# Ring slots released on read, S5 preparation between projections, and a blocked DeltaNet inverse

## The chip, the cores and the metric

One core of one Trainium2 chip runs the whole layer in one launch. The metric is the device time of that core in microseconds (us). The kernel before has a median of 3605.3 us over 3 runs (3603.2 to 3605.53).

## The reference, cut to what matters

The program is one layer on 256 tokens of width 2048, all in float32: a token mixer, a layer norm, a mixture of 32 experts and a second layer norm.

```
proj   = x @ w_in                                   # S5 input u, q, k, v, z, beta/decay, two gates
y_s5   = glu(gelu(diagonal state scan(u)))          # 128 groups, 64 states, (y@w_glu_a)*sigmoid(y@w_glu_b)
q,k,v  = silu(conv4(...)); q,k normalised
lower  = I + strict_tril((k*beta) k^T * decay)      # per head and chunk
sol    = lower^-1 [v*beta, k*beta*exp(g)]           # triangular solve
o      = chunked delta rule with state S; o = rmsnorm(o)*norm_w*silu(z);  y_dn = o @ w_dn_out
mix    = (gate_s5*y_s5 + gate_dn*y_dn) @ w_mix_out
h      = layer_norm(ALPHA*x + mix);  out = layer_norm(ALPHA*h + experts(h))
```

## The kernel before, in words

Activations stand transposed in SBUF (`xT`: 16 tiles of 128 by 256 tokens). Nearly all weights stream through a **ring of three slots** of 2 MB (`ring`, 16 by 256 columns a partition). SyncE issues every load, in one hand-written order. `load_slot` (its call site is L300 in the profile) waits until a PSUM bank that an earlier slot filled has been *taken* by VectorE or ScalarE, then issues. On TensorE `project`/`part` (L553) wait for slot and bank and multiply 32 tiles of 128x128 with 256 tokens. Each float32 matmul is two load-and-multiply pairs of instructions, so a slot is 64 of each.

The order of the stages:

- **Prologue.** Six loads count on one semaphore, `pro_loaded`, and TensorE waits for all six before its transposes of x (L528). Then come beta and decay logits (L533), a chain over VectorE and ScalarE that ends in `glog_ready`, two sums (L538, L539), and `prologue_done`, after which group 0 starts.
- **DeltaNet groups.** A loop of 8, each with 4 value heads and two chunks of 128 tokens (`c` = 0, 1). TensorE projects q, k and half of v (the front), and spreads the other half of v (slot 0), z0 (slot 1) and z1 (slot 2) over the waits of the rest. The inverse of `lower` is built by doubling over `LEVELS` = 7 levels: P = At·Ti (L609) into one bank per chunk, VectorE masks it to `Pm` (L1258), X = Tt·Pm (L616) and Pm·Tt (L618), VectorE subtracts both from `Ti` (L1262) and `Tt` (L1264). Each level works on full 128x128 blocks of 4 heads; two z0 matmuls stand after P and one z1 matmul after X. Then the inverse is applied (L630 to L655) and the output is normalised (L661).
- **S5 input and preparation.** All engines meet at `phase_done[0]`. Only then SyncE issues the S5 parameters and the first three of 8 u slots (copied out at L1027). After the last u slot VectorE prepares the state matrices (L1298 to L1374), TensorE transposes them in 16 banks of four (L692) and ScalarE copies them (L1050 to L1052).
- **Scan.** Four chunks of 64 steps. TensorE forms the inputs (L703, tiles of 32 rows), ScalarE spreads them, VectorE steps the state (L1397 to L1403), TensorE forms the outputs (L734). The gate and output projections of DeltaNet run on TensorE beside the scan (L553, L721).
- **GLU.** 8 iterations of three slots in banks 0, 1, 2. ScalarE takes two sigmoids (L1083, L1085), VectorE three products and sums (L1435 to L1441).
- **Mix.** After `phase_done[2]`, 8 slots of `w_mix` (L762), with x, the norm rows and the first expert units loaded between.
- **Router and experts.** 16 expert pairs joined in tiles of 64 columns (L849 to L907), with six 2 MB units in flight. The diff has no line in it.

Of the kernel before, what the change touches and what calls it, by code (L numbers as in the profile page):

```python
# [18 lines left out]
P = 128  # L19
# [9 lines left out]
LEVELS = 7  # L29
OFF_Q = 2048  # L30
# [37 lines left out]
def build(nc, x, w_in, conv_w, a_log, dt_bias, norm_w, w_dn, lam_re, lam_im, log_dt, b_re, b_im, c_re, c_im,  # L68
# [3 lines left out]
    with ExitStack() as ctx:  # L72
# [148 lines left out]
        turn_begun = sem("turn_begun")  # L221
# [24 lines left out]
        s5_loaded, s5_tr, s5_trc, s5_step = sem("s5_loaded"), sem("s5_tr"), sem("s5_trc"), sem("s5_step")  # L246
        uch_ready = sem("uch_ready")
# [39 lines left out]
        def _(sp):  # L287

            sp.dma_start(xtok, x[0].rearrange("(m p) d -> p m d", p=P)).then_inc(pro_loaded, 16)
            sp.dma_start(wbd, in_rows(w_in[:, OFF_BD:OFF_BD + 2 * H_V])).then_inc(pro_loaded, 16)  # L290
            sp.dma_start(cw[:, :, :], conv_w.rearrange("(j p) t -> p j t", p=P)).then_inc(pro_loaded, 16)
            sp.dma_start(arow, a_log.partition_broadcast(P)).then_inc(pro_loaded, 16)
            sp.dma_start(dtrow, dt_bias.partition_broadcast(P)).then_inc(pro_loaded, 16)
            sp.dma_start(normw, norm_w.rearrange("(p o) -> p o", o=1)).then_inc(pro_loaded, 16)

            def load_slot(buf, src, bank, taken):
# [5 lines left out]
            with sp.Fori(0, GROUPS) as g:  # L302
                for r, col in enumerate((OFF_Q + 256 * g, OFF_K + 256 * g, OFF_V + 512 * g, OFF_V + 256 + 512 * g,
                                         OFF_Z + 512 * g, OFF_Z + 256 + 512 * g)):
                    load_slot(r % RING, in_rows(w_in[:, ds(col, SC)]), r % 3, 2 * g + r // 3 + 1)
# [12 lines left out]
            with sp.Fori(0, 2) as q:
                for r in range(3):
                    load_slot((S_U + r) % RING, in_rows(w_in[:, ds(768 * q + 256 * r, SC)]), r, U_USE + q + 1)  # L320
            for r in range(6, 8):
                load_slot((S_U + r) % RING, in_rows(w_in[:, SC * r:SC * r + SC]), r % 3, U_USE + 3)
            with sp.Fori(0, 8) as c:
                load_slot(S_DN % RING, in_rows(w_in[:, ds(OFF_GDN + SC * c, SC)]), 0, DN_USE + 1 + c)
# [1361 lines left out]
```

## Time and profile before

| What | Value |
|---|---|
| median of 3 runs | 3605.3 us |
| profiled execution | 3604.39 us |
| its span | 3602.3 us |
| TensorE matmul busy | 3206.1 us (89%) |
| VectorE busy | 1047.1 us (29%) |
| ScalarE busy | 482.2 us (13%) |
| mean read from HBM | 183 GB/s |

The profiled execution has 2.1 us around its span. A line such as L553 is a line of the kernel before; a helper's line stands for all its callers. A busy TensorE can still be waiting within a matmul's modelled end, so stage lengths are read from start times.

### The profile page before, as it was taken

The numbers are of one execution on the slowest core, as the hardware profiler recorded it, in microseconds if no ns is written. First come the engines' busy times: TensorE is split into PE (matmuls) and PEld (weight loads), VectorE is DVE, ScalarE is ACT, GpSimd is POOL, SyncE is SP. The second block draws the span as 40 slices with busy tenths as digits, with TensorE's granted clock in tenths as the row PEclk, the third lists the DMA queues.
The fourth block names the chain that finished last, engine by engine and source line by source line (L and its number), as shares of the span: only waits on it lengthen the run. The fifth ranks groups of instructions, "written<-read, shape, count | busy, mean of one in ns | idle before, by whom it ended". The sixth has DMA issues, their size and how long they took to land.

```text
span 3602.3 us, 44020 instructions
## 1 busy us (share of the span) xinstructions
PE 3206.1 (89%) x17395; PEld 2437.7 (68%) x17395; DVE 1047.1 (29%) x2650; ACT 482.2 (13%) x632; POOL 106.8 (3%) x189
## 2 busy tenths in 40 slices
PE   6999999999997868787788787895899999999996
PEld 6988888888886757676676676685545445454542
DVE  1433433433423026465570000003111111121114
ACT  1121121121121021101100000000011101111111
POOL 1010010010010000000000000000000000000000
PEclk9999999999999888798898998897899999999998
DMA  5232232242230622232223334273499999999995
GB/s 148 71 116 93 70 116 70 80 130 70 70 116 9 178 94 94 68 99 83 80 94 117 97 113 140 87 275 117 192 406 410 396 409 396 410 409 396 409 396 212
DMA packets 325973, 660.87 MB, mean 183 GB/s; under 512 B 41840, under 2 KB 271344, under 8 KB 275440
## 3 DMA queue, kind: packets, MB, share of 16 engines
q1 hardware_dynamic: 325904, 659.85, 49.9%
q8 instruction: 56, 0.92, 0.1%
q14 instruction: 13, 0.11, 0.0%
HBM read 657.73 MB, written 2.10 MB: 183 GB/s over the span
## 4 chain that ended last, share of the span: by engine, by line
PE 60%; issue 16%; DVE 9%; DVEq 5%; DMA 3%; ACT 2%; SPq 1%; ACTq 1%; POOL 1%; POOLq 1%
PE bank L553 17%; PE bank L860 12%; PE bank L849 6%; PE bank L891 6%; PE bank L907 3%; PE bank L618 3%; PE bank L616 3%; PE bank L762 2%; DVE arena L1401 2%; DVE arena L1403 2%; PE bank L609 2%; DVEq L1400 2%; DMA arena<-in_w_glu_a_dram 2%; PE bank L734 1%; PE bank L703 1%
## 5 line engine op out<-in xcount | busy, mean ns | idle before, releaser
L553 PE MATMUL bank<-arena 128*128 128x256 f32 x5632 | 1285.1, 387 | 117.3 <-DMA arena<-in_w_glu_a_dram 71.0
L553 PEld LDWEIGHTS bank<-arena 128*128 128x128 f32 x5632 | 1081.0, 195 | 274.3 <-issue 90.4
L860 PE MATMUL bank<-arena 128*64 128x512 f32 x2048 | 442.2, 592 | 0.7 <-ACT arena L1119 0.7
L860 PEld LDWEIGHTS bank<-arena 128*64 128x64 f32 x2048 | 147.1, 137 | 292.5 <-issue 290.5
L721 PE MATMUL bank<-arena 128*128 128x256 f32 x1024 | 229.1, 387 | 19.9 <-DMA arena<-in_w_dn_out_dram 19.9
L849 PEld LDWEIGHTS bank<-arena 128*128 128x128 f32 x1024 | 224.8, 311 | 15.4 <-issue 12.2
L721 PEld LDWEIGHTS bank<-arena 128*128 128x128 f32 x1024 | 198.8, 195 | 49.5 <-DMA arena<-in_w_dn_out_dram 16.0
L849 PE MATMUL bank<-arena 128*128 128x128 f32 x1024 | 227.8, 384 | 3.1 <-DVEq L1594 3.1
L891 PE MATMUL bank<-arena 128*64 128x512 f32 x1024 | 223.3, 594 | 7.7 <-ACT arena L1129 7.7
L891 PEld LDWEIGHTS bank<-arena 128*64 128x64 f32 x1024 | 72.2, 137 | 148.4 <-issue 137.0
L1629 DVE TENSOR_TENSOR arena<-arena,bank 128x512 f32<-128x512 f32 x128 | 87.7, 687 | 198.6 <-PE bank L907 198.5
L1600 DVE TENSOR_TENSOR arena<-bank,arena 128x512 f32<-128x512 f32 x16 | 11.1, 692 | 458.6 <-PE bank L860 458.6
L609 PE MATMUL bank<-arena 128*128 128x128 f32 x896 | 123.9, 281 | 7.8 <-DVEq L1253 3.9
L762 PE MATMUL bank<-arena 128*128 128x256 f32 x512 | 115.4, 390 | 12.6 <-DMA arena<-in_w_mix_out_dram 12.6
L609 PEld LDWEIGHTS bank<-arena 128*128 128x128 f32 x896 | 112.4, 191 | 21.0 <-DVEq L1266 13.1
L1435 DVE TENSOR_TENSOR arena<-arena,bank 128x512 f32<-128x512 f32 x8 | 5.5, 689 | 413.9 <-ACTq L1086 413.9
L762 PEld LDWEIGHTS bank<-arena 128*128 128x128 f32 x512 | 100.3, 196 | 27.7 <-issue 13.3
L618 PE MATMUL bank<-arena 128*128 128x128 f32 x896 | 118.3, 275 | 0.0
L616 PE MATMUL bank<-arena 128*128 128x128 f32 x896 | 118.2, 275 | 0.0
L907 PE MATMUL bank<-arena 128*128 128x512 f32 x256 | 115.2, 593 | 2.5 <-DVEq L1613 1.8
L1262 DVE TENSOR_TENSOR arena<-arena,bank 128x512 f32<-128x512 f32 x112 | 77.1, 688 | 137.7 <-PE bank L618 137.7
L616 PEld LDWEIGHTS bank<-arena 128*128 128x128 f32 x896 | 113.3, 192 | 2.9
(277 smaller groups left out, 2264.7 us busy)
## 6 DMA issues: line engine op xcount, KB each, us to landing
arena<-in_w_in_dram SPq DMA_DIRECT2D x72, 2048.0 KB, 8.4
arena<-in_w_gate_dram SPq DMA_DIRECT2D x64, 2048.0 KB, 16.3
arena<-in_w_up_dram SPq DMA_DIRECT2D x64, 2048.0 KB, 13.3
arena<-in_w_down_dram SPq DMA_DIRECT2D x64, 2048.0 KB, 19.2
arena<-in_w_dn_out_dram SPq DMA_DIRECT2D x16, 2048.0 KB, 11.3
arena<-in_w_glu_a_dram SPq DMA_DIRECT2D x8, 2048.0 KB, 8.3
arena<-in_w_glu_b_dram SPq DMA_DIRECT2D x8, 2048.0 KB, 13.7
arena<-in_w_mix_out_dram SPq DMA_DIRECT2D x8, 2048.0 KB, 11.1
```

The lines of the kernel that those rows point to most:

```text
L553: last = mm(ps[bank][:, ct * T:ct * T + T], ring[:, buf, k, ct * P:ct * P + P], rhs[:, k, :], start=k == 0, stop=k == KD - 1)
L609: last = mm(ps[3 + 2 * c][:, a * P:a * P + P], At[:, c, a], Ti[:, c, a], start=True, stop=True)
L616: mm(ps[3 + 2 * c][:, a * P:a * P + P], Tt[:, c, a], Pm[:, c, a], start=True, stop=True)
L618: last = mm(ps[4 + 2 * c][:, a * P:a * P + P], Pm[:, c, a], Tt[:, c, a], start=True, stop=True)
L721: last = mm(ps[1][:, ct * T:ct * T + T], ring[:, buf, k, ct * P:ct * P + P], oT[:, half * KD + k, :], start=half == 0 and ct == 0 and k == ...
L762: last = mm(ps[bank][:, m * SC:m * SC + SC], mg[:, k, m * P:m * P + P], ring[:, buf, k, :], start=k == 0, stop=k == KD - 1)
L849: last = mm(ps[4 + b][:, k * P:k * P + P], h1[:, m, 4 * b + k::KD], Psel[:, m].rearrange("p o c -> p (o c)"), start=m == 0, stop=m == MT - 1)
L860: last = mm(ps[bank][CAP * o:CAP * o + CAP, :], xg[:, 4 * q + k, CAP * o:CAP * o + CAP], w[:, o, k], start=q == 0 and k == 0, stop=q == 3 ...
L891: last = mm(ps[4 + n][CAP * o:CAP * o + CAP, :], shT[:, k, CAP * o:CAP * o + CAP], unit[j % UNITS][:, o, n * 512:n * 512 + 512], start=k = ...
L907: last = mm(ps[(2, 3, 0, 1)[n % 4]][:, :], pwT[:, (n // 4) * P:(n // 4) * P + P], ysb[:, (n % 4) * 512:(n % 4) * 512 + 512], start=True, s ...
L1262: V.tensor_tensor(Ti[:, c], Ti[:, c], ps[3 + 2 * c][:, :].rearrange("p (a t) -> p a t", a=GV), ALU.subtract)
L1629: V.tensor_tensor(av, av, ps[(2, 3, 0, 1)[n % 4]][:, :], ALU.add).then_inc(sc_taken, 1)
```

## The change

- **Loads.** `load_slot` waits on `bank_ready` (the slot has been read) in place of `bank_taken`. x comes in two loads, then the logit weights and the first three ring slots, then biases, conv weights and norm weight, each with its own semaphore. The S5 parameters are issued before the u slots, during the last group; the C matrices after `phase_done[0]`. The first `w_dn` slot of each pair is released at half through `half_read`. Three `w_mix` slots are issued before `phase_done[2]`.
- **TensorE order.** Group 0's first projection runs ahead of the decay sums, which move to bank 7. The u slots follow the last group without the meeting of all engines. The S5 transposes stand between u slots 1 and 2, 5 and 6, 6 and 7.
- **Inverse.** Six levels work on the two 64x64 diagonal blocks, of which `Ti`, `Tt`, `Pm` keep only 64 columns; the seventh fills the off-diagonal block of a full `TtF`. A `sem_inc` of `solve_begun` stands after each wait.
- **GLU.** Even and odd iterations use banks 0 to 2 and 3 to 5.

```
@@ sync
-            sp.dma_start(xtok, ...).then_inc(pro_loaded, 16)      # and wbd, cw, arow, dtrow, normw
+            for m in range(MT):
+                sp.dma_start(xtok[:, m], xv[:, m]).then_inc(x0_loaded, 16)
+            sp.dma_start(wbd, ...).then_inc(wbd_loaded, 16)
+            for r in range(3):
+                sp.dma_start(ring[:, r], ...).then_inc(slot_loaded[r], 16)
+            sp.dma_start(dtrow, ...).then_inc(bias_loaded, 16)
+            sp.dma_start(arow, ...).then_inc(bias_loaded, 16)
+            sp.dma_start(cw[:, :, :], ...).then_inc(pro_loaded, 16)
+            sp.dma_start(normw, ...).then_inc(pro_loaded, 16)
-                sp.wait_ge(bank_taken[bank], taken)
+                sp.wait_ge(bank_ready[bank], read)
                 sp.sem_inc(load_free, 1)
...
-            sp.wait_ge(phase_done[0], 4)
             (lam_re, lam_im, log_dt, b_re, b_im, d_skip loads)
+            for r in range(3):
+                load_slot((S_U + r) % RING, ..., r, U_USE)
+            sp.wait_ge(phase_done[0], 4)
             (c_re, c_im loads)
+            for r in range(3, 8):
+                load_slot((S_U + r) % RING, ..., r % 3, U_USE + r // 3)
...
+            with sp.Fori(1, 8) as c:
+                load_glu(c)
+            for r in range(2):
+                load_slot((S_MIX + r) % RING, ..., r, MIX_USE[r])
+            load_slot((S_MIX + 2) % RING, ..., 2, MIX_USE[2])
             sp.wait_ge(phase_done[2], 4)
@@ tensor
-            pe.wait_ge(pro_loaded, 96)
-            pe.wait_ge(const_ready, 1)
+            pe.wait_ge(ident_ready, 1)
+            pe.wait_ge(x0_loaded, 32)
...
+            project(16, 0, 0, 0, xT)
+            pe.wait_ge(const_ready, 1)
+            pe.wait_ge(glog_ready, 1)
+            mm(ps[7][:, 0:64], upper, small[:, 128:192], start=True, stop=True)
+            mm(ps[7][:, 64:96], ones[:, :], glog[:, 0], start=True, stop=True).then_inc(gcum_ready, 1)
+            project(16, 1, 1, 0, xT)
+            project(16, 2, 2, 0, xT)
+            with pe.Fori(0, GROUPS - 1) as g:
+                group(g)
+                front(g + 1)
+            group(GROUPS - 1)
...
+                for lv in range(HALF_LEVELS):
                     for c in range(2):
                         pe.wait_ge(t_ready[c], 8 * g + lv + 1)
+                        pe.sem_inc(solve_begun, 1)
                         for a in range(GV):
-                            last = mm(ps[3 + 2 * c][:, a * P:a * P + P], At[:, c, a], Ti[:, c, a], ...)
+                            for b in (lower, higher):
+                                last = mm(ps[3 + 2 * c][b, a * HB:a * HB + HB], At[b, c, a, b], Ti[b, c, a], ...)
                         last.then_inc(p_ready[c], 1)
                     z0(16 + 2 * lv, 18 + 2 * lv)
                     for c in range(2):
                         pe.wait_ge(pm_ready[c], 7 * g + lv + 1)
+                        pe.sem_inc(solve_begun, 1)
                         (the same halving for Tt·Pm and Pm·Tt: 16 products of 64x64 for 8 of 128x128)
+                    z1(lv, lv + 1)
+                lv = HALF_LEVELS
+                (per chunk 4 products P of At[lower, .., higher]·Ti[lower], z0 x2, 4 products Pm[higher]·TtF[higher], z0 x2)
...
+            u_slot(0)
+            pe.wait_ge(o_ready, GROUPS)
+            pe.sem_inc(phase_done[0], 1)
+            u_slot(1)
+            pe.wait_ge(s5_lam_loaded, 48)
+            pe.wait_ge(s5_step, 1)
+            (3 transposes of spar)
+            for r in range(2, 6):
+                u_slot(r)
+            turn_wide(0, bwide, 2)
+            u_slot(6)
+            turn_wide(1, cwide, 3)
+            u_slot(7)
...
+            with pe.Fori(0, 4) as q:
+                for odd in range(2):
+                    glu_slot(2 * q + odd, 0, 0, GLU_USE, uT, odd)
+                    glu_slot(2 * q + odd, 1, 1, GLU_USE, uT, odd)
+                    glu_slot(2 * q + odd, 2, 2, GS5_USE, xT, odd)
@@ vector
-                for lv in range(LEVELS):
+                for lv in range(HALF_LEVELS):
...
-                        V.tensor_tensor(Ti[:, c], Ti[:, c], ps[3 + 2 * c][:, :]..., ALU.subtract)
-                        V.tensor_tensor(Tt[:, c], Tt[:, c], ps[4 + 2 * c][:, :]..., ALU.subtract)
+                        V.tensor_tensor(Ti[:, c], Ti[:, c], heads(3 + 2 * c), ALU.subtract)
+                        if lv < HALF_LEVELS - 1:
+                            V.tensor_tensor(Tt[:, c], Tt[:, c], heads(4 + 2 * c), ALU.subtract)
+                        else:
+                            for b in (lower, higher):
+                                V.tensor_tensor(TtF[b, c, :, b], Tt[b, c], heads(4 + 2 * c)[b], ALU.subtract)
                         dve.drain()
                         dve.sem_inc(t_ready[c], 1)
+                lv = HALF_LEVELS
+                (copy Pm[higher] out of PSUM; TtF[lower, c, :, higher] = -heads(4 + 2 * c)[lower])
```

`heads(bank)` is the first 256 columns of a bank as 4 heads of 64. `glu_slot` is `project` with bank `3 * odd + b` and a wait for `bank_taken` one iteration older. `turn_wide` holds the 32 transposes of one of the two matrices, as L692 before. ScalarE's copies (`take_u`, `take_wide`) follow the same order.

## Rows read from the trace of the kernel before

**Rows 1.** Windows by stage: us, busy (x count) per engine, PEclk, DMA share, GB/s

```profile
0.00:40.95 40.95, 13.80 (x100) 13.36 (x101) 4.27 (x11) 10.35 (x16) 9.17 (x42) 0.94 0.81 222
40.95:84.95 44.00, 44.00 (x193) 38.34 (x193) 6.98 (x16) 4.49 (x5) 7.16 (x14) 0.94 0.30 96
638.33:776.68 138.35, 136.78 (x815) 122.24 (x814) 54.27 (x100) 28.06 (x33) 12.13 (x18) 1.00 0.28 91
1150.30:1187.75 37.45, 0.14 (x1) 0.00 (x0) 2.73 (x3) 3.96 (x5) 0.00 (x0) 0.57 0.66 123
1187.75:1336.84 149.09, 122.92 (x580) 108.36 (x580) 22.52 (x47) 15.21 (x29) 0.00 (x0) 0.90 0.44 139
1336.84:1908.66 571.82, 454.32 (x3585) 400.59 (x3585) 331.44 (x1311) 78.00 (x86) 0.00 (x0) 0.86 0.28 89
1908.66:2333.90 425.24, 354.25 (x1536) 306.00 (x1536) 14.52 (x21) 19.16 (x23) 0.00 (x0) 0.90 0.33 104
...
2344.34:2462.20 117.86, 115.41 (x512) 100.23 (x512) 4.81 (x7) 0.00 (x0) 0.00 (x0) 0.96 0.68 245
...
2547.70:3602.30 1054.60, 1011.42 (x4448) 502.46 (x4448) 196.60 (x366) 125.54 (x199) 0.00 (x0) 0.99 0.93 379
```

**Rows 2.** Timeline of TensorE in the prologue: start us, us, operation, idle before

```profile
18.66 5.38 PE L528 MATMUL bank<-ident,arena 128*128 128x128 f32 x32 [18.66 <-DMA small<-in_dn_norm_w_dram]
24.82 7.36 PE L533 MATMUL bank<-arena 128*128 128x64 f32 x64 [0.79 <-DVE arena L1175]
38.31 0.69 PE L538 MATMUL bank<-small,masks 128*128 128x64 f32 x2 [6.13 <-DVEq L1189]
```

**Rows 3.** DMA issues in the first 60 us: count, KB, us to landing

```profile
arena<-in_w_in_dram SPq DMA_DIRECT2D x3, 2048.0 KB, 14.8
arena<-in_x_dram SPq DMA_DIRECT2D x1, 2048.0 KB, 7.6
```

**Rows 4.** Timeline of TensorE in the inverse of group 4

```profile
672.78 2.29 PE L609 MATMUL bank<-arena 128*128 128x128 f32 x16
674.91 1.03 PE L553 MATMUL bank<-arena 128*128 128x256 f32 x4
675.77 1.05 PE L616 MATMUL bank<-arena 128*128 128x128 f32 x8
...
679.78 2.30 PE L609 MATMUL bank<-arena 128*128 128x128 f32 x16
...
707.79 2.29 PE L609 MATMUL bank<-arena 128*128 128x128 f32 x16
...
715.97 1.13 PE L630 MATMUL bank<-arena 128*128 128x128 f32 x8 [0.59 <-issue]
```

**Rows 5.** Timeline of VectorE in group 4

```profile
648.23 0.42 DVE L1238 COPY arena<-bank 128x256 f32<-128x256 f32 x1 [2.88 <-PE bank L571]
...
677.76 0.69 DVE L1262 TENSOR_TENSOR arena<-arena,bank 128x512 f32<-128x512 f32 x1 [1.96 <-PE bank L618]
```

**Rows 6.** Timeline of TensorE where it works on part of the array

```profile
1336.84 2.01 PE L703 MATMUL bank<-masks,arena 32*128 32x64 f32 x64 [2.48 <-DVE masks L1384]
...
2562.64 27.69 PE L860 MATMUL bank<-arena 128*64 128x512 f32 x128 [0.68 <-ACT arena L1119]
...
2589.73 0.60 PE L860 MATMUL bank<-arena 128*64 128x512 f32 x2
2590.26 1.57 PE L849 MATMUL bank<-arena 128*128 128x128 f32 x6
```

**Rows 7.** Timeline of TensorE: S5 transposes, and one scan output

```profile
1325.05 9.31 PE L692 MATMUL bank<-ident,arena 128*128 128x128 f32 x64 [23.69 <-DVEq L1370]
...
1609.15 12.42 PE L734 MATMUL bank<-arena 128*32 128x64 f32 x256 [9.53 <-DVEq L1407]
```

**Rows 8.** Waits from 1908 to 2463 us: us in total, times, longest

```profile
PE bank L553 <- DMA arena<-in_w_glu_a_dram: 71.0, 7, 10.3
...
PE bank L762 <- DMA arena<-in_w_mix_out_dram: 12.6, 2, 10.2
```

More of the change, by code:

```diff
@@ L29 @@
 LEVELS = 7
+HALF_LEVELS = 6
+HB = 64
 OFF_Q = 2048
@@ L294, in _, with load_slot @@
-            sp.dma_start(normw, norm_w.rearrange("(p o) -> p o", o=1)).then_inc(pro_loaded, 16)
-            def load_slot(buf, src, bank, taken):
-                sp.wait_ge(bank_taken[bank], taken)
+            def load_slot(buf, src, bank, read):
+                sp.wait_ge(bank_ready[bank], read)
                 sp.sem_inc(load_free, 1)
                 sp.dma_start(ring[:, buf], src).then_inc(slot_loaded[buf], 16)
[L302 to L305, printed above, removed]
@@ L318, in _ @@
[L318 to L324, printed above, removed]
-                for h in range(2):
-                    load_slot((S_DN + 1 + h) % RING, tile_rows(w_dn[h * D:h * D + D, ds(SC * c, SC)]), 1,
-                              DN_USE + 1 + c)
@@ new lines, in load_gdn, with load_dn_second @@
+            def load_gdn(c, bank, read):
+                load_slot(S_DN % RING, in_rows(w_in[:, ds(OFF_GDN + SC * c, SC)]), bank, read)
+            def load_dn_second(c, read):
+                load_slot((S_DN + 2) % RING, tile_rows(w_dn[D:2 * D, ds(SC * c, SC)]), 1, read)
+            load_gdn(0, 2, U_USE + 2)
+            load_slot((S_DN + 1) % RING, tile_rows(w_dn[0:D, 0:SC]), 0, U_USE + 3)
+            load_dn_second(0, U_USE + 3)
+            with sp.Fori(1, 8) as c:
+                load_gdn(c, 0, DN_USE + c)
+                sp.wait_ge(half_read, c)
+                sp.sem_inc(load_free, 1)
+                sp.dma_start(ring[:, (S_DN + 1) % RING], tile_rows(w_dn[0:D, ds(SC * c, SC)])).then_inc(
+                    slot_loaded[(S_DN + 1) % RING], 16)
+                load_dn_second(c, DN_USE + c)
@@ L466, in _ @@
             pool.drain()
+            for b in range(2):
+                rows = slice(HB * b, HB * b + HB)
+                g.tensor_copy(half_mask[rows], level_mask[rows, 0:HALF_LEVELS, HB * b:HB * b + HB])
+                g.tensor_copy(half_ident[rows], ident[rows, HB * b:HB * b + HB])
+            pool.drain()
+            g.memset(TtF, 0.0)
             g.tensor_copy(halfmask[:, 1:2], level_mask[:, 4, 0:1])
@@ L629, in _ @@
                 for a in range(GV):
-                    last = mm(ps[3][:, a * P:a * P + P], Tt[:, 0, a], vtok[:, 0, a], start=True, stop=True)
+                    last = mm(ps[3][:, a * P:a * P + P], TtF[:, 0, a], vtok[:, 0, a], start=True, stop=True)
                 last.then_inc(apply_pe, 1)
@@ L648, in _ @@
                 for a in range(GV):
-                    last = mm(ps[3][:, a * P:a * P + P], Tt[:, 1, a], R[:, a], start=True, stop=True)
+                    last = mm(ps[3][:, a * P:a * P + P], TtF[:, 1, a], R[:, a], start=True, stop=True)
                 last.then_inc(apply_pe, 1)
```

262 lines of the change are left out of this document (161 added, 101 removed).

## The prediction

> **What bounds the kernel now.** I cut the span by stage first (the windows view). In the group loop TensorE is busy 136.8 of a period of 138.35 us at the full clock of 2.4 GHz, VectorE 54.3 and ScalarE 28.1 [rows 1]: TensorE's own work is the bound there, eight times. Where the change moves loads it is not: TensorE stands still for 37.45 us before the u slots, is busy 122.9 of 149.1 us in S5 input and preparation, and 354 of 425 us in the GLU [rows 1]. In the scan TensorE waits for VectorE's last step (9.53 us before an output burst [rows 7]), so work taken from TensorE there buys nothing. The experts move 379 GB/s with DMA busy 0.93 and TensorE 1011 of 1055 us [rows 1]; no line of the diff is in them.
>
> The sum is made against the profiled execution's 3604.4 us, 0.9 below the median of the three runs and 2.1 above its span. A measurement here can tell about 0.2% (7 us) from no change.
>
> **Price of a slot.** Four L553 instructions take 674.91 to 675.77, 0.215 us each [rows 4]; 64 make 13.8 us.
>
> **1. Prologue, -19 us.** TensorE starts at 18.66 because the last of six loads lands then [rows 2]. x itself needs 7.6 us [rows 3]; issued first, it lets the transposes begin at about 8.5. They hand over after 6.2 us and the logits take 7.4 [rows 2], ending at 22.1. Group 0's first slot fills 22.1 to 35.9. The decay chain (32.2 to 38.3 before, 6.1 us [rows 2]) now also needs the biases, which queue behind x, the logit weights and three ring slots. Three ring slots took a median of 14.8 us to land [rows 3]; streamed behind the others I estimate the biases at 31.5, so the chain ends near 37.6 and TensorE stands 1.7 us. Two more slots end near 66; before, the front ended at 84.95 [rows 1]. Bounds: 22 us if the biases come sooner; 9 if they and the conv weights come 10 us later. Cover: the first slot hides most of the chain; without it 6 us come back. VectorE's new wait for conv weights and norm weight holds only conv(0), and group 0 needs that at 66.
>
> **2. Inverse, -140 us.** *One level before* is 672.78 to 679.78, 7.0 us. Its 48 instructions of 128 columns take 0.11 us each (8 of L616 in 1.05 with the last one's end), 5.35 us in all, plus 1.3 for three z matmuls (six instructions) [rows 4]. *After*, 96 instructions of 64 by 64 stand in place of the 48. The trace has none of that shape. The nearest: 64 instructions of 32 rows and 64 columns in 2.01 us including the last one's end, so about 0.028 each [rows 6]. One pass of 64 columns at a quarter of L553's 0.215 is 0.054, so two run at a time. The column tiles of L860 say the same: 128 in 27.69, 0.216 each, half the time of 512 columns [rows 6]. Both have float32's two passes on one tile before the next tile, exactly the order of the new loops. So the low end is 0.028 and the high end 0.056 (no overlap); I take 0.028, as both rows agree: 2.7 us for 5.35.
>
> *Switch of tile shape*, four times a level. From the last L860 pair to L849 is 0.53 us where a pair takes 0.43 [rows 6]: 0.1 us. The Trainium skill, TensorEngine Tiling (Key Properties), says that changing the tiling mode drains TensorE. By a whole drain, taken as the 0.16 us by which the L609 burst's end outlasts the next start (2.29 against 2.13 [rows 4]) on each of the four switches and on top of the row's 0.1, a level would be up to 0.3 longer and the total up to 14 us higher; the row has a drain of 0.1 at most.
>
> *VectorE* works on 256 columns: 0.42 us for 0.69 [rows 5]. Walking the chain (P of chunk 0, 0.45; about 0.4 until VectorE starts, which began at 677.76, 0.2 after X's last issue [rows 4, 5]; mask 0.42, covered by z0; X 0.9 a chunk; again 0.4; two subtracts 0.8, covered by X of chunk 1 and z1) the work on TensorE is 2.7 + 1.3 + 0.4 = 4.4 and the waits for `t_ready` leave 0.3: 4.7 us a level, 2.3 saved, six times. The new `sem_inc`s put the waits on TensorE's sequencer; what is queued behind each is the next burst, whose issue the z matmuls hide, except P of chunk 1: from nothing to 0.2 us a level, I take nothing. *Last level*: P and X are four products a chunk on one tile, 0.9 us each pair of chunks, four z0 matmuls 1.7, switches 0.4, so 4.0 against 707.79 to 715.97, 8.2 us [rows 4]; the two half-height writes of `TtF` give 0.5 back: 3.7 saved. Together 13.8 + 3.7 = 17.5 a group, 140 in eight. Low end of saving 10 (serial passes), high end 165 (no switch, no wait). What is late next is nothing else: a group of 121 us still holds VectorE's under 50 and 12 MB of slots, 100 GB/s against the 245 that the mix stage moves [rows 1]. The apply steps keep their full 128x128 form.
>
> **3. Meeting and S5 preparation, -65.5 us.** Before: 37.45 + 149.09 = 186.5 us from the last group to the first scan input [rows 1]. After: the first u slots are loaded during group 7, because bank 0, 1, 2 are ready there; all SyncE work ahead of them (parameters, many small rows) sits in the 70 us in which z0 and z1 are consumed. 8 slots are 110.4; 64 transposes took 9.31, partly at 1.2 GHz [rows 7], I take 8; ScalarE and VectorE hand over in 2 (2.48 before [rows 6]); sum 121 with the three small ones. VectorE's 24 us preparation (23.69 [rows 7]) lies beside slots 2 to 5 (55 us); without that cover it would return. The C loads stand ahead of u slot 3 on SyncE: a few us of issue against 13.8 x 3 = 41 us until slot 3 is wanted. Bounds: 55 to 70.
>
> **4. Scan, 0.** Earlier `w_dn` and gate slots end TensorE's waits on DMA, but VectorE ends last [rows 7]. Between -5 and +5.
>
> **5. GLU, -91 us.** 425.2 us hold seven waits for `w_glu_a` of 10.2 us, 71 together [rows 8], and a clock of 0.90 [rows 1]: after each stop TensorE restarts at 1.2 GHz. After, a slot is refilled as soon as it is read, 27.6 us before it is wanted, against 14.8 us even for three queued [rows 3]; 6 MB in 41.4 us are 152 GB/s. The second bank set keeps the sigmoids off TensorE's path. 24 slots are 331 us, and 3 for the restart after the GELU: 334. Bounds: 75 to 93.
>
> **6. Mix, -14 us.** 2333.90 to 2462.20 is 128.3 us. Three slots are now resident when all engines meet; the hand-over by one sigmoid and three vector operations is near 3.8, and 8 slots are 110.4: 114.2. x, norm rows and two units (8 MB) now stand ahead of slot 3, wanted 41 us later. Bounds: 5 to 16.
>
> Sum: 19 + 140 + 65.5 + 0 + 91 + 14 = 329.5; 3604.4 - 329.5 = **3275 us**.
>
> **Rivals.** *A. Diagonal pairs do not overlap* (chance 0.14). L703's row tiles write four different banks and L860's column tiles share their rows; a pair in two row tiles writing one bank is in no row. Serial, 96 x 0.056 = 5.4, plus z and switches, gives 7.3 a level: the six levels lose 2 us a group and the last gains 3.7, 10 to 15 in all, so 3275 + 127 = 3402. A half-way rate (0.042, level near 6) gives 3335. The Trainium skill, TensorEngine Tiling (Gotcha 1: PSUM Pressure), says that different row tiles cannot access the same bank at once and software must keep them apart, which speaks against this part of the change; by it the time would be rival A's. *B. The ring still starves in the GLU* (0.06): if refills come no sooner than before, the 71 us of waits and the clock loss stay: 3275 + 88 = 3363. Against it: 10.2 us a wait equals a load issued after the bank was taken. *C. Slower* (0.03): the granted clock falls to 1.2 GHz in the inverse, since each pass fills half the array, and stays low after it. A microsecond of TensorE work then costs two. All savings are gone when 330 / 8 = 41 us of each group run so, the 32 us of the inverse and 9 after it; with 45 it is 3275 + 360 = 3635. Against it: TensorE hardly stops there, and L703's and L860's partial tiles ran at the full rate. *D. Part 1 or 3 does not happen* because a load lands late behind the new order (0.05): up to 3275 + 65 = 3340.
>
> **How the numbers follow.** The forecast has 0.72. Its own bounds are 3250 (high ends of 2 and 3) to 3310 (a switch of 0.25 and sequencer waits). Reaching to the half-way rate of A, to B and to D gives 3240 to 3375; full A, C and the unforeseen are left out, under 0.2. Faster 0.96, same 0.01, slower 0.03 (C).
>
> **What would show it.** Group 0's norm sums (L564 before) at 66 us; group period 121 us, level 4.7; instructions of 64x64 every 0.028 us on average; no stop between group 7 and the u slots; scan beginning 121 us after them; scan unchanged at 572; GLU 334 with no wait for `w_glu_a`; mix 114; experts 1055. A period above 130, a GLU above 350, or a clock under 0.95 in the group loop makes it wrong.

## The result, and the profile after

| | before | after |
|---|---|---|
| median of four runs each, same chip | 3605.1 us | 3280.9 us (3278.0 to 3287.3) |
| profiled execution (span) | 3604.4 us (3602.3) | 3282.5 us (3280.6) |

The ratio is 0.9104, 95% interval 0.9093 to 0.9115: about 9% less time. The forecast was 3275 in 3240 to 3375.

The windows view of the changed kernel. It has one row for each stage: prologue and first front, group loop, u slots with S5 preparation, scan, GLU, mix, rest. Columns: from:to and length, busy time (x instructions) of TensorE, its weight loads, VectorE, ScalarE, GpSimd, then granted clock, DMA share, GB/s.

```profile
0.00:65.70 65.70, 55.51 (x292) 50.09 (x293) 11.33 (x27) 14.85 (x20) 17.89 (x60) 1.00 0.73 203
65.70:1004.70 939.00, 927.76 (x8497) 788.29 (x8496) 336.24 (x782) 215.62 (x255) 83.96 (x130) 1.00 0.33 103
1004.70:1124.40 119.70, 118.25 (x582) 104.20 (x581) 25.25 (x50) 18.78 (x34) 0.00 (x0) 1.00 0.48 150
1124.40:1689.80 565.40, 444.54 (x3585) 394.63 (x3585) 329.79 (x1311) 78.00 (x86) 0.00 (x0) 0.85 0.29 94
1689.80:2022.90 333.10, 333.10 (x1536) 292.84 (x1536) 14.51 (x21) 14.00 (x19) 0.00 (x0) 1.00 0.45 145
2022.90:2138.90 116.00, 112.49 (x514) 98.38 (x512) 6.88 (x10) 1.88 (x2) 0.76 (x4) 0.99 0.64 235
2138.90:3280.60 1141.70, 1050.37 (x4573) 529.69 (x4572) 233.04 (x449) 133.74 (x214) 0.00 (x0) 0.95 0.87 355
```

TensorE is now busy 118.25 of 119.7 us between the last group and the scan, and all of the GLU, both at a granted clock of 1.00. The scan keeps its old clock, 0.85 against 0.86 [rows 1]; the rest, which the change leaves alone, is at 0.95. Read from start to start, the 321.7 us between the two spans fall apart so:

| stage | before | after | forecast | measured |
|---|---|---|---|---|
| to group 0's norm sums | 84.95 | 65.72 | -19 | -19.2 |
| eight groups | 1065.3 | 939.0 | -140 | -126.3 |
| u slots and S5 preparation | 186.5 | 119.6 | -65.5 | -66.9 |
| scan | 571.8 | 565.4 | 0 | -6.4 |
| GLU | 425.2 | 333.2 | -91 | -92.0 |
| mix | 128.3 | 116.0 | -14 | -12.3 |
| rest | 1140.1 | 1141.7 | 0 | +1.6 |

**The inverse.** TensorE's timeline in group 4 (start, us, line, shape, count, idle before): the first level, a middle level, the last. It answers to [rows 4].

```profile
583.28 0.68 PE L655 MATMUL bank<-arena 64*64 64x64 f32 x16
584.82 0.68 PE L655 MATMUL bank<-arena 64*64 64x64 f32 x16 [0.86 <-DVEq L1356]
...
593.91 1.15 PE L655 MATMUL bank<-arena 64*64 64x64 f32 x32
594.99 1.13 PE L595 MATMUL bank<-arena 128*128 128x256 f32 x4
596.05 0.68 PE L664 MATMUL bank<-arena 64*64 64x64 f32 x16
596.57 0.63 PE L668 MATMUL bank<-arena 64*64 64x64 f32 x16
597.03 0.63 PE L664 MATMUL bank<-arena 64*64 64x64 f32 x16
597.50 0.63 PE L668 MATMUL bank<-arena 64*64 64x64 f32 x16
598.07 0.70 PE L595 MATMUL bank<-arena 128*128 128x256 f32 x2
598.70 1.15 PE L655 MATMUL bank<-arena 64*64 64x64 f32 x32
...
613.03 0.67 PE L677 MATMUL bank<-arena 64*64 64x64 f32 x8
614.25 0.65 PE L677 MATMUL bank<-arena 64*64 64x64 f32 x8 [0.54 <-DVEq L1375]
...
617.92 1.05 PE L694 MATMUL bank<-arena 128*128 128x128 f32 x8
```

From one burst of 16 to the next inside X it is 596.57 to 597.03 and 597.03 to 597.50: 0.465 / 16 = 0.029 us an instruction, so the diagonal tiles do run two at a time. A middle level is 593.91 to 598.70, 4.78 us on average for 7.0 before, without a stop. Its sum: 96 x 0.029 = 2.80, six z instructions 1.30, and 0.68 is left for four changes of tile shape, 0.17 each on average.

**The other stages**, timeline of TensorE again: the prologue (against [rows 2]), the preparation between u slots, and the joins of scan, GLU and mix.

```profile
8.56 6.15 PE L575 MATMUL bank<-ident,arena 128*128 128x128 f32 x32 [8.56 <-DMA arena<-in_x_dram]
...
37.57 0.41 PE L730 MATMUL bank<-small,masks 128*128 128x64 f32 x2 [0.85 <-DVEq L1290]
...
1004.75 27.79 PE L595 MATMUL bank<-arena 128*128 128x256 f32 x128
1032.47 0.39 PE L761 MATMUL bank<-ident,arena 64*128 64x64 f32 x3
1032.80 55.52 PE L595 MATMUL bank<-arena 128*128 128x256 f32 x256
1088.15 3.66 PE L751 MATMUL bank<-ident,arena 128*128 128x128 f32 x32
...
1689.79 333.33 PE L831 MATMUL bank<-arena 128*128 128x256 f32 x1536 [7.40 <-ACTq L1174]
2026.63 112.46 PE L852 MATMUL bank<-arena 128*128 128x256 f32 x512 [3.51 <-DVEq L1568]
```

None of the three preparation steps (L761 once, L751 twice) has an idle time in a bracket, and none of the 24 GLU slots has one inside the stage: the 7.40 us stand before its first slot, at the join with the scan. Before, the GLU had seven waits for weights [rows 8].

### The profile page after: what moved, and what is told of

The parts are those of the page before. It is cut to its first block, busy times and chain, and to the rows that moved or that the text cites. A ratio compares the mean times of both kernels' runs of the same rounds, so it can differ in the third digit from the quotient of the medians.

```text
span 3280.6 us, 48447 instructions
## 1 busy us (share of the span) xinstructions
PE 3042.0 (93%) x19571; PEld 2258.1 (69%) x19571; DVE 957.1 (29%) x2650; ACT 476.9 (15%) x628; POOL 102.6 (3%) x194
## 4 chain that ended last, share of the span: by engine, by line
PE 64%; issue 16%; DVE 9%; DVEq 4%; ACT 2%; ACTq 1%; POOL 1%; POOLq 1%; SPq 1%; DMA 0%
PE bank L950 13%; PE bank L831 10%; PE bank L595 9%; PE bank L939 7%; PE bank L981 7%; PE bank L852 3%; PE bank L997 3%; DVE arena L1519 2%; DVE arena L1521 2%; DVEq L1518 2%; PE bank L811 2%; PE bank L655 1%; PE bank L664 1%; PE bank L778 1%; PE bank L668 1%
## 5 line engine op out<-in xcount | busy, mean ns | idle before, releaser
L595 PE MATMUL bank<-arena 128*128 128x256 f32 x4096 | 937.1, 384 | 0.0
L595 PEld LDWEIGHTS bank<-arena 128*128 128x128 f32 x4096 | 770.0, 191 | 114.0 <-issue 7.7
L831 PE MATMUL bank<-arena 128*128 128x256 f32 x1536 | 333.3, 380 | 7.4 <-ACTq L1174 7.4
L831 PEld LDWEIGHTS bank<-arena 128*128 128x128 f32 x1536 | 292.9, 191 | 47.8 <-issue 7.7
L939 PEld LDWEIGHTS bank<-arena 128*128 128x128 f32 x1024 | 224.7, 311 | 15.4 <-issue 12.2
L939 PE MATMUL bank<-arena 128*128 128x128 f32 x1024 | 227.8, 384 | 3.1 <-DVEq L1718 3.1
L796 PE MATMUL bank<-arena 128*128 128x256 f32 x1024 | 222.3, 379 | 0.0
L796 PEld LDWEIGHTS bank<-arena 128*128 128x128 f32 x1024 | 194.6, 190 | 26.5
L981 PEld LDWEIGHTS bank<-arena 128*64 128x64 f32 x1024 | 72.4, 138 | 149.9 <-issue 138.4
L1753 DVE TENSOR_TENSOR arena<-arena,bank 128x512 f32<-128x512 f32 x128 | 87.7, 687 | 198.7 <-PE bank L997 198.5
L852 PE MATMUL bank<-arena 128*128 128x256 f32 x512 | 112.5, 383 | 3.5 <-DVEq L1568 3.5
L811 PE MATMUL bank<-arena 128*32 128x64 f32 x1024 | 51.7, 381 | 67.1 <-DVEq L1525 67.1
L852 PEld LDWEIGHTS bank<-arena 128*128 128x128 f32 x512 | 98.4, 192 | 17.6 <-DVEq L1568 3.9
L1312 DVE TENSOR_SCALAR arena<-bank,cw 128x256 f32<-128x256 f32 x64 | 28.0, 479 | 254.8 <-PE bank L595 254.2
L1555 DVE TENSOR_TENSOR arena<-arena,bank 128x512 f32<-128x512 f32 x8 | 5.5, 688 | 321.7 <-ACTq L1182 321.7
L778 PE MATMUL bank<-masks,arena 32*128 32x64 f32 x1024 | 52.3, 383 | 47.8 <-ACTq L1160 46.3
L811 PEld LDWEIGHTS bank<-arena 128*32 128x32 f32 x1024 | 47.5, 145 | 70.6 <-DVEq L1525 67.9
## 6 DMA issues: line engine op xcount, KB each, us to landing
arena<-in_w_down_dram SPq DMA_DIRECT2D x64, 2048.0 KB, 19.2
```

Source lines behind the costliest of these rows:

```text
L595: last = mm(ps[bank][:, ct * T:ct * T + T], ring[:, buf, k, ct * P:ct * P + P], rhs[:, k, :], start=k == 0, stop=k == KD - 1)
L778: last = mm(ps[4 + i][:, k * STEPS:k * STEPS + STEPS], BT[32 * i:32 * i + 32, c, kh * 8 + k, :], uch[32 * i:32 * i + 32, kh * 8 + k, :], s ...
L796: last = mm(ps[1][:, ct * T:ct * T + T], ring[:, buf, k, ct * P:ct * P + P], oT[:, half * KD + k, :], start=half == 0 and ct == 0 and k == ...
L811: last = mm(ps[2 + k // 8][32 * i:32 * i + 32, (k % 8) * STEPS:(k % 8) * STEPS + STEPS], CT[:, c, k, 32 * i:32 * i + 32], SS[:, 1:STEPS + ...
L831: last = mm(ps[3 * odd + b][:, ct * T:ct * T + T], ring[:, buf, k, ct * P:ct * P + P], rhs[:, k, :], start=k == 0, stop=k == KD - 1)
L852: last = mm(ps[bank][:, m * SC:m * SC + SC], mg[:, k, m * P:m * P + P], ring[:, buf, k, :], start=k == 0, stop=k == KD - 1)
```

## The experiments

Twelve kernels ran, each beside the kernel before on its own chip. Chips differ by some 5 us in that kernel, so an experiment stands to the changed kernel by ratios: (its ratio - 0.9104) x 3603 us. The interval of a ratio is about 0.0015 to either side, 5 us; for the difference of two kernels it is about 7 us.

### Undoing one part

**Inverse put back.** The six half levels and the last one are replaced by the old loop, in TensorE's and VectorE's code, with the old buffers:

```diff
-for lv in range(HALF_LEVELS):
...
-    last = mm(ps[3 + 2 * c][b, a * HB:a * HB + HB], At[b, c, a, b], Ti[b, c, a],
+for lv in range(LEVELS):
...
+    last = mm(ps[3 + 2 * c][:, a * P:a * P + P], At[:, c, a], Ti[:, c, a],
```

> The changed kernel with the inverse alone put back to seven levels on 128x128 tiles, its buffers and its VectorE steps too. My theory: of the 321.7 us between the two profiled spans, 126 come from the inverse (group loop end 1004.75 against the sum with the old levels), so this kernel takes 3281 + 126 = 3407 us (3400 to 3415), group period 138.3 us, level 7.0 us, last level 8.2. Rival: the 126 also holds something the other parts gave to the group loop (slots released on read, new order of the loads); then this kernel takes clearly less than 3400, and the group period stays under 137.

Measured 3405.9 us, ratio 0.9462 (0.9446 to 0.9478): +129. The group period is 138.4 us in place of 122.6, which makes 15.8 x 8 = 126.5. The group loop's gain is the inverse's alone; slots released on read gave nothing there.

**Diagonal tiles in rows.** Each tile gets all its products in a row, so that the overlap that rival A of the prediction denies is taken away on purpose:

```diff
-for a in range(GV):
-    for b in (lower, higher):
+for b in (lower, higher):
+    for a in range(GV):
```

In X both sets of one block stand before both of the other.

> Same products as the changed kernel, but within a burst all products of the lower diagonal block are issued first, then all of the higher, so that neighbours in the queue no longer sit on different row and column groups. Theory: a 64x64 product costs 0.029 us only because its neighbour runs on the other diagonal tile at the same time; in a row on one tile each costs 0.058 us, the 48 instructions of P (two chunks, 32 x 2... 64 in all) and the 128 of X cost twice as much, level 4.8 -> 7.3 us or a little less, some 2.5 x 6 x 8 = 120 us more, 3400 us. Rival: the queue finds the pair anyway, or 0.058 is no matter of overlap; then the time stays at 3281 and the level at 4.8.

Measured 3357.4 us, ratio 0.9326 (0.9310 to 0.9342): +80. The theory holds in kind, its size was too high. Timeline of TensorE in one level of this kernel:

```profile
628.90 1.54 PE L655 MATMUL bank<-arena 64*64 64x64 f32 x32
630.36 1.13 PE L595 MATMUL bank<-arena 128*128 128x256 f32 x4
631.42 0.68 PE L664 MATMUL bank<-arena 64*64 64x64 f32 x8
631.94 0.45 PE L667 MATMUL bank<-arena 64*64 64x64 f32 x5
...
635.39 1.54 PE L655 MATMUL bank<-arena 64*64 64x64 f32 x32
```

P now takes 1.46 us to the next start instead of 1.08, and the level 6.5 instead of 4.8 (1.7 x 48 = 82). Single starts show why it is not doubled: products on one tile follow each other after 0.058 us, but where the block changes the first three or four of the other tile start beside the last of this one (626.435, 626.441, 626.494, 626.548, 626.552 us). The last products of one tile start after the first of the next (626.494 after 626.441), so some work is taken out of its order, but only three or four instructions of it. Pairs side by side in the program get all of the overlap, pairs 8 or 16 apart only that at the seams. What sets this reach is not shown.

**Two more changes of tile shape a level.**

```diff
 for c in range(2):
...
     last.then_inc(p_ready[c], 1)
-z0(16 + 2 * lv, 18 + 2 * lv)
+    z0(16 + 2 * lv + c, 17 + 2 * lv + c)
```

> Same work as the changed kernel; in each of the six levels the two z products that stood together between P and X stand one behind the P burst of each chunk, so a level has two more changes of tile shape (into 128x128 and back), 96 of them over the kernel. Theory: a change costs 0.14 us into 64x64 and 0.20 us back, measured as gaps in the stream; 0.34 x 48 = 16 us more at most, less what had been a wait on VectorE: 3281 + 12 = 3293 us (3289 to 3298), level 4.8 -> 5.05. Rival 1: the gaps are filled time, the level is set by the VectorE chain: no change (3281). Rival 2: the switch drains the array fully and costs 0.5 us or more: above 3305.

Measured 3291.2 us, ratio 0.9145 (0.9130 to 0.9160): +15, within the forecast and between its two rivals. One level:

```profile
593.52 0.68 PE L655 MATMUL bank<-arena 64*64 64x64 f32 x16
594.13 0.70 PE L595 MATMUL bank<-arena 128*128 128x256 f32 x2
594.76 0.68 PE L655 MATMUL bank<-arena 64*64 64x64 f32 x16
...
598.64 0.56 PE L655 MATMUL bank<-arena 64*64 64x64 f32 x12
```

593.52 to 598.64 is 5.12 us against 4.78: 0.34 for one change into 64x64 and one back, as in the changed kernel's own rows.

**GLU slots released when the bank is taken**, as before; both bank sets stay.

```diff
-load_slot(S_GLU % RING, tile_rows(w_glu_a[:, ds(SC * c, SC)]), 0, GLU_USE + c)
+load_taken(S_GLU % RING, tile_rows(w_glu_a[:, ds(SC * c, SC)]), 0, GLU_USE + c + 1)
```

`load_taken` is `load_slot` with a wait for `bank_taken`; the other two slots of a turn likewise.

> In the GLU stage alone a weight slot's reload again waits until the results of its last use have been read out of PSUM (bank taken), as before the change; the two sets of PSUM banks stay. Theory: the release on read is what removed the waits on w_glu_a and the stops of TensorE with them; putting it back returns most of the 92 us, 3281 + 85 = 3366 us (3350 to 3375), GLU stage about 418 us, w_glu_a waits of 10 us each again and a granted clock that drops after them. Rival: the double PSUM set was what did it, or the loads' order; then the stage stays within 15 us of 333.

Measured 3368.6 us, ratio 0.9357 (0.9342 to 0.9373): +91. First the GLU on TensorE's timeline, then its waits (total, times, longest) and a window of it:

```profile
1739.67 44.32 PE L837 MATMUL bank<-arena 128*128 128x256 f32 x192 [10.49 <-DMA arena<-in_w_glu_a_dram]
1794.42 5.83 PE L837 MATMUL bank<-arena 128*128 128x256 f32 x14 [10.43 <-DMA arena<-in_w_glu_a_dram]
...
PEld bank L837 <- DMA arena<-in_w_glu_a_dram: 76.1, 7, 10.9
...
1940.00:1990.00 50.00, 39.51 (x173) 34.00 (x172) 2.07 (x3) 1.19 (x2) 0.00 (x0) 0.90 0.39 126
```

The waits are back, and with them the clock of 0.90. A turn of three slots is 1739.67 to 1794.42, 54.75 us: 41.65 as in the changed kernel, 10.66 of stop, and 2.44 for the clock. Seven stops and eight times the last are 94 us, and the stage is 94 longer. Undoing the release alone takes back the stage's whole gain of 92 us, although the second bank set is still there.

**One set of GLU banks**, with the release on read kept.

```diff
-pe.wait_ge(bank_taken[b], uses + c)
+pe.wait_ge(bank_taken[b], uses + c + 1)
...
-    last = mm(ps[3 * odd + b][:, ct * T:ct * T + T], ring[:, buf, k, ct * P:ct * P + P], rhs[:, k, :],
+    last = mm(ps[b][:, ct * T:ct * T + T], ring[:, buf, k, ct * P:ct * P + P], rhs[:, k, :],
```

> In the GLU stage one set of three PSUM banks instead of two, so TensorE starts a bank's next projection only when its last result has been taken; weight slots are still released on read. Theory: the release on read carries nearly all of the 92 us; the second set of banks is worth only the stop at each of the 7 turns in which TensorE waits for the two gates and one multiply (some 1.8 us from the last product to the bank's release): 3281 + 13 = 3294 us (3288 to 3300) against this chip's level of the changed kernel. Rival: without the second set the read releases come late enough that the loads fall behind again, 3281 + 50 or more, and w_glu_a waits appear.

Measured 3295.2 us, ratio 0.9142 (0.9127 to 0.9158): +14. TensorE stops 1.56 us at a turn (timeline row below), seven of which are 11 us; no wait for weights appears. The two parts depend on each other: with the old release the second bank set is worth nothing that can be measured (92 - 91), with the new one 14. So the two are not added.

```profile
1740.03 35.23 PE L831 MATMUL bank<-arena 128*128 128x256 f32 x162 [1.56 <-DVEq L1556]
```

**The meeting before the u slots, and the preparation behind them.** Two kernels:

```diff
-u_slot(0)
 pe.wait_ge(o_ready, GROUPS)
 pe.sem_inc(phase_done[0], 1)
+pe.wait_ge(phase_done[0], 4)
+u_slot(0)
...
+sp.wait_ge(phase_done[0], 4)
 sp.dma_start(spar[0:NJ, 0, :], lam_re.rearrange("(j g) n -> j (g n)", g=2)).then_inc(s5_lam_loaded, 16)
```

```diff
 u_slot(1)
+for r in range(2, 8):
+    u_slot(r)
 pe.wait_ge(s5_lam_loaded, 48)
...
-for r in range(2, 6):
-    u_slot(r)
 turn_wide(0, bwide, 2)
-u_slot(6)
 turn_wide(1, cwide, 3)
-u_slot(7)
```

In the second, ScalarE's copies follow the same order.

> The changed kernel with the meeting of all engines before the u slots put back: TensorE waits for the last group's output and for all engines before the first u slot, and the loads of the S5 parameters and of the u slots are issued only after it. The S5 preparation stays between the projections. Theory: of the 66.9 us between group 7's end and the scan's start some 37 come from the missing meeting (the wait for the normed output and for the u weights, which then arrive behind the S5 loads), so 3281 + 37 = 3318 us (3308 to 3328). Rival: nearly all comes from the preparation between the projections; then this kernel is within 15 us of 3281.

> The changed kernel with all S5 transposes and their ScalarE copies behind the eight u slots, as before the change; loads and the missing meeting stay. Theory: the preparation is no longer covered by projections, 3281 + 28 = 3309 us (3300 to 3320), group end to scan some 148 us instead of 119.6, nearly all of it waits of TensorE for the S5 chain on VectorE. Together with the meeting alone (37) that is the 66.9 us. Rival: since the loads come early now, VectorE's chain ends before the u slots do, and the order matters only for the 16 transposed blocks' copies: +15 or less.

Measured 3317.7 us, ratio 0.9208 (0.9193 to 0.9224), +37 for the meeting; 3307.9 us, ratio 0.9181 (0.9166 to 0.9197), +28 for the order. Both land on the theory, and together they are 65 of the stage's 66.9. One row of each shows what is paid: the wait for the first u slot's weights, and the wait for VectorE's preparation without its cover.

```profile
1037.87 29.88 PE L595 MATMUL bank<-arena 128*128 128x256 f32 x128 [34.03 <-DMA arena<-in_w_in_dram]
```

```profile
1139.22 8.72 PE L751 MATMUL bank<-ident,arena 128*128 128x128 f32 x64 [23.67 <-DVEq L1480]
```

**The old prologue.**

```diff
-pe.wait_ge(ident_ready, 1)
 pe.wait_ge(x0_loaded, 32)
+pe.wait_ge(wbd_loaded, 16)
+pe.wait_ge(bias_loaded, 32)
+pe.wait_ge(pro_loaded, 32)
+pe.wait_ge(const_ready, 1)
...
-project(16, 0, 0, 0, xT)
...
+pe.wait_ge(prologue_done, 1)
+project(16, 0, 0, 0, xT)
 project(16, 1, 1, 0, xT)
```

SyncE loads x, `wbd`, `cw`, `arow`, `dtrow` and `normw` again before the three ring slots.

> The changed kernel with the old prologue: small parameters loaded ahead of the first three weight slots, TensorE waits for all of them and for the constants before its first transpose, the decay sums and the wait for the prologue's end stand before the first projection. Theory: the prologue's term alone, 3281 + 19 = 3300 us (3296 to 3303), norm sums of group 0 at 84 to 85 us instead of 65.7, nothing later changed. Rival: a later load order makes up for part of it (less than +12), or the order of loads alone explains it.

Measured 3302.3 us, ratio 0.9160 (0.9144 to 0.9175): +20. The norm sums of group 0 start at 86.17, 20.5 later than in the changed kernel. The order of the loads and the order of TensorE's work were put back together, so this does not say what each is worth. 129 + 91 + 37 + 28 + 20 are 305 of the 322 us. The mix (12.3) was not undone by itself, so its cause is read from the timeline only.

### Towards a faster kernel

**Signals of the inverse.** The two stops in the first and last level (0.86 and 0.54 us above) come from VectorE signalling late, behind work whose results TensorE does not need yet.

```diff
 for c in range(2):
     dve.wait_ge(kq_ready, 2 * g + c + 1)
-    dve.wait_ge(dm_ready, 2 * g + c + 1)
+    dve.wait_ge(dexp_ready, 2 * g + c + 1)
...
-    V.tensor_tensor(attn[:, c].rearrange("p (b r) t -> p b r t", r=2),
...
+        if lv == 0:
+            attn_of(c)
         dve.wait_ge(p_ready[c], 7 * g + lv + 1)
```

`attn_of` waits for `dm_ready` and forms attn. In the sixth level `sem_inc(t_ready[c], 1)` stands before the writes of `TtF`. TensorE waits for `dm_ready` once before the first level, since it reads GpSimd's identities there.

> The changed kernel with two waits of the inverse taken off TensorE's path: VectorE forms At of both chunks first and signals each at once (attn, which needs GpSimd's Dm, is formed behind), and in the sixth level it signals after Ti, before the two half-height writes of TtF. Theory: TensorE's stops of 0.86 us before the second P of the first level and 0.54 us before the second of the last level go, 8 times: 3281 - 11 = 3270 us (3267 to 3276), the first level 5.0 us instead of 5.85 and the last 4.35 instead of 4.89. Rival: attn, now in front of the first level's masks, moves the same stop to the X burst; then 3278 to 3282.

Measured 3266.3 us, ratio 0.9071 (0.9059 to 0.9084): -12. The first level is now 575.74 to 580.52, 4.78 us like every other, the last 604.42 to 608.73, 4.31:

```profile
575.74 1.15 PE L656 MATMUL bank<-arena 64*64 64x64 f32 x32
...
604.42 1.27 PE L678 MATMUL bank<-arena 64*64 64x64 f32 x16
...
608.73 1.05 PE L695 MATMUL bank<-arena 128*128 128x128 f32 x8
```

**Two engines fill the scan's buffer.**

```diff
-for i in range(4):
+for i in range(2):
     nc.scalar.copy(view[:, kh, c, i], ps[4 + i][:, :].rearrange("p (k t) -> p k t", k=8))
...
+for i in range(2, 4):
+    V.tensor_copy(view[:, kh, c, i], ps[4 + i][:, :].rearrange("p (k t) -> p k t", k=8))
```

> The changed kernel with the scan's inputs copied out of PSUM by two engines: ScalarE takes banks 4 and 5, VectorE, which is idle there, banks 6 and 7. Theory: each of the 16 rounds of copies is 3.6 us long now and stands between two input bursts of 3.7 us; with two copies on each engine it is 1.8 us, 16 x 1.8 = 29 us less: 3252 us (3247 to 3260), scan stage 536 instead of 565, period of a chunk 130.5. Rival: the two engines read PSUM at the cost of each other (copies of 1.3 us instead of 0.9 and 0.7), or VectorE's copies with strides of the scan's buffer are slow: less than half of it, above 3267.

Measured 3257.8 us, ratio 0.9051 (0.9035 to 0.9067): -19, two thirds of the 29. Timeline of ScalarE, then VectorE, in the second chunk's fill:

```profile
1259.90 1.87 ACT L1161 COPY arena<-bank 128x512 f32<-128x512 f32 x2 [26.96 <-PE bank L813]
...
1271.85 2.36 ACT L1161 COPY arena<-bank 128x512 f32<-128x512 f32 x2 [4.45 <-PE bank L780]
...
1260.00 1.87 DVE L1510 COPY arena<-bank 128x512 f32<-128x512 f32 x2 [7.66 <-PE bank L813]
...
1271.85 2.37 DVE L1510 COPY arena<-bank 128x512 f32<-128x512 f32 x2 [4.19 <-PE bank L780]
```

In nine of the 16 rounds both engines start at the same moment, and there each pair of copies takes 2.4 us instead of 1.87: the rival was right for part, some 5 of the missing 10 us, and the rest is within the interval. Overlap alone is not enough: at 1259.90 and 1260.00 the two start 0.10 us apart, run side by side, and take 1.87 each. Whether PSUM or the buffer side does it was not tried.

**Both edits in one kernel.**

> Both edits, signals of the inverse and shared copies. They lie in different stages and share nothing but VectorE's queue: the gains add, 3281 - 11 - 29 = 3241 us (3235 to 3250), ratio to the kernel before 0.899.

Measured 3247.7 us, ratio 0.9022 (0.9010 to 0.9035): -30 where the two alone gave 31, so they add; the forecast of 41 carried the shared fill's 10 too many.

**TensorE kept working through its waits in the scan**, on top of both:

```diff
+def busy(n):
+    for _ in range(n):
+        mm(ps[0][:, :], ones[:, :], xT[:, 0:2, :].rearrange("p k t -> p (k t)"), start=True, stop=True)
...
+if r > 0:
+    busy(2)
 pe.wait_ge(bu_taken, 4 * ch + r + 1)
...
+busy(16)
 pe.wait_ge(scan_done, ch + 1)
```

> The kernel with both edits, and in the scan stage TensorE does not stand still while it waits: 2 products of 128x512 into a free bank ahead of each of the three later input bursts, 16 ahead of each y burst (0.43 us an instruction, two instructions each, so about 1.7 and 13.7 us, inside waits of 2.4 to 3.4 and 14.6 to 17 us). Their results are overwritten unread. Theory: an input burst takes 3.69 us at a granted clock of 0.50 and 2.01 at 1.00 (both stand in the changed kernel's trace); kept at 1.00, the 12 later bursts give 12 x 1.68 = 20 us, and the y bursts, which start at 0.5 and rise within 4 us, some 2 us each, 8: 3248 - 28 = 3220 us (3212 to 3232). Rival 1: the clock falls between the bursts all the same, or a burst's pace is set by the issue of small products and not by the clock: 3243 or more. Rival 2: the fillers run longer than the waits and delay the bursts: above 3252.

Measured 3237.3 us, ratio 0.8984 (0.8971 to 0.8996): -14 against the kernel with both edits, half of what was expected. Windows over an input burst of the changed kernel and then of this one (the number behind GpSimd's is the granted clock):

```profile
1270.40:1274.10 3.70, 3.68 (x64) 3.50 (x64) 0.00 (x0) 0.00 (x0) 0.00 (x0) 0.50 0.02 4
```

```profile
1255.20:1257.20 2.00, 1.97 (x65) 1.93 (x65) 0.00 (x0) 0.00 (x0) 0.00 (x0) 1.00 0.00 0
```

and this kernel's timeline from the y burst to the fillers behind it:

```profile
1230.41 13.92 PE L823 MATMUL bank<-arena 128*32 128x64 f32 x256 [3.70 <-DVEq L1559]
1247.02 3.59 PE L777 MATMUL bank<-arena,ones 128*128 128x512 f32 x4 [2.69 <-issue]
```

The input bursts do what the theory said: 64 instructions in 2.01 us at 2.4 GHz instead of 3.69 at 1.2. The y bursts do not. They kept 12.5 to 13.9 us. A second set of windows shows that the clock is not what holds them: four microseconds hold as few of their instructions at 1.00 as at 0.65, some 0.056 us from start to start in both. The counts of these rows include a few that began before the window.

```profile
1230.40:1234.40 4.00, 3.99 (x71) 3.69 (x74) 3.67 (x1) 0.00 (x0) 0.00 (x0) 0.65 0.02 4
1234.40:1238.40 4.00, 4.00 (x79) 3.62 (x73) 4.00 (x1) 0.00 (x0) 0.00 (x0) 1.00 0.01 4
1238.40:1244.30 5.90, 5.90 (x123) 5.24 (x115) 0.49 (x1) 0.00 (x0) 0.00 (x0) 1.00 0.01 3
```

So rival 1 holds for the y bursts, which are paced by something else than the clock. The VectorE column of these rows has one instruction, and it is a suspect that was not tried. VectorE's timeline has it in the first row; its source line in the second (eight times, shortest, median and longest in ns):

```profile
1230.73 8.15 DVE L1563 TENSOR_TENSOR arena<-bank,arena 128x512 f32 x1 [0.41 <-issue]
...
L1563 DVE TENSOR_TENSOR arena<-bank,arena x8: 691/2428/8155, 1179.8 to 1627.0; 128x512 f32 x6, 128x512 f32<-128x512 f32 x2
```

The four of the eight outside the y bursts take 0.69 us; the four inside take 4.2 to 8.2. After the 8.15 us one has ended, the burst's pace at the same clock of 1.00 is near 0.05 us. So the two seem to hold each other up. It cannot be all: in the kernel with one set of GLU banks, one y burst kept 0.058 us for 10 us after VectorE's instruction had ended, at a clock of 1.00. The fillers behind this y burst run at a clock of 0.53 after a 2.69 us stop and hold the next input burst up. This is the fastest kernel measured, 43 us under the changed one.

## Why the prediction was right

**Prologue, 19: right** (19.2), and for its reason: VectorE took up the biases at 31.38 us, forecast 31.5, and the chain's stop is 0.85 us instead of 1.7. **Meeting and preparation, 65.5: right** (66.9), in both halves. **GLU, 91: right** (92.0), and for its reason, the load one bank hand-over earlier. **Mix, 14:** 12.3; TensorE stands 3.51 us at the join against 3.8 foreseen, but the eight slots take 112.5 to the end of the last instead of 110.4. After the join TensorE ran its first 6.4 us at a mean granted clock of 0.73, a restart that the sum had for the GLU and not here.

**Inverse, 140: right in mechanism, 14 too high.** Three terms of "4.7 us a level, six times, 3.7 saved in the last" were mis-sized. A change of tile shape was put at 0.1 us, from a row where the tiles change their columns only; it measures 0.17, so four cost 0.68 instead of 0.4 a level. The 0.3 us of waits for `t_ready` that stood beside it do not exist in the middle levels, which is why 4.78 came so near 4.7. In the first level the waits do exist: I counted it like the others, though it begins behind VectorE's At and attn and GpSimd's mask; it is 5.85 us and saved 1.57 instead of 2.3. In the last level the two half-height writes, charged at 0.5, cost a stop of 0.54; without the stop it is 4.31 us (the signals' experiment) where 4.0 was foreseen, mostly the changes of tile shape again, so it saved 3.3 instead of 3.7. 1.57 + 5 x 2.22 + 3.3 = 16.0 a group against 17.5. The signals' experiment gave 1.65 of it back in every group.

**Scan, 0:** -6.4, a microsecond and a half outside its bounds. Where it lies is seen: of the three turns between chunks before, two had some 2.2 us more of stop between the y burst and the next input burst than the third (6.12 and 5.94 us against 3.79), and after the change all three are like the third, which is 4.4; the four y bursts together are 51.7 us after against 53.5, which is 1.7. Why is open: no line of these bursts was changed. The two long stops are the turns of TensorE's loop (the third leaves it), and the DMA moved 335 and 295 GB/s in them, against 4 GB/s in the same places after the change. That loads delay the loop's turn fits this and was not tried. The y bursts vary by themselves: over the experiments that left the scan alone one took from 11.8 to 15.4 us, in no order. The argument for 0 was too strong as well. It said that work taken from TensorE buys nothing there, because VectorE ends last; the shared copies (19 us) and the input bursts at full clock (14 us) show that the rounds that fill the buffer are on the path too.

**The total** is nearer than its largest term. The inverse fell 13.7 us short, and the scan's 6.4 us, which no reasoning foresaw, made good nearly half of it. That part is luck.

**Rivals.** A was refuted: the pairs overlap. Its price for a product without overlap was right (0.058 us on one tile, 0.056 foreseen), and in the wrong order 80 us return, not 127. B needed refills no sooner than before; made so, the GLU paid 91. C did not happen: the group loop's granted clock is 1.00, with the 64x64 products in it. D did not happen either.

On the rule that software must keep row tiles off the same bank (the Trainium skill, TensorEngine Tiling (Array Packing), Gotcha 1: PSUM Pressure): both diagonal tiles write one bank here, one its partitions 0 to 63 and the other 64 to 127, and ran two at a time, 0.029 us against 0.058 in a row. For tiles that differ in rows and columns the rows decide against it; tiles that differ in rows alone were not tried. The drain that the same page of the Trainium skill names under Key Properties shows here as 0.17 us a change on average.

## What to carry to other kernels

Release a buffer on the event that frees it, its last read, and not on the one that proves the result safe: with a ring of three slots and a second set of banks, undoing this one edit cost 91 us. When work is split into small array tiles, put products of different tiles next to each other in the program, and count every change of tile shape. And read the first and the last pass of a loop by themselves: they have other neighbours than the middle ones, and 1.6 us a group lay there.

## What was not expected of the hardware

- Two products on diagonal 64x64 tiles start 6 ns apart and the next pair 58 ns after; an order that puts 8 or 16 on one tile first still overlaps three or four at each seam, and no more.
- After a stop of 3.7 us the next input burst ran wholly at 1.2 GHz, and useless products of nearly 2 us inside each stop kept it at 2.4.
- ScalarE and VectorE copying 128x512 out of PSUM to one buffer took 2.4 us a pair instead of 1.87 where they started at the same moment, and 1.87 where they started 0.10 us apart.
- Bursts on 128x32 tiles ran at some 0.05 us an instruction and did not follow the clock, while those on 32x128 tiles took 0.031 us at 2.4 GHz and 0.058 at 1.2.
- A VectorE instruction that takes 0.69 us by itself took 3.4 to 8.2 us beside those 128x32 bursts.
